# Two heads at a time in the attention stage of a two-layer transformer kernel

## Chip, core and metric

The kernel runs on one NeuronCore of one Trainium2 chip. The metric is the device time of one execution in microseconds (us). The whole model is one program; the input is one sequence of 512 tokens with 1024 features, everything in 32-bit floats.

## What is computed

Two layers of a block (feed-forward, token mixing, feed-forward), then a third block of another kind, which the change does not touch. Inside the token mixing of each layer stand two attentions over the same 512 tokens. Cut to what matters here:

```python
def masked_softmax(scores, mask):
    s = jnp.where(mask, scores.astype(jnp.float32), -jnp.inf)
    m = jnp.max(s, -1, keepdims=True)
    p = jnp.exp(s - m)
    return p / jnp.maximum(jnp.sum(p, -1, keepdims=True), 1.0)

# nsa_attention: 8 query heads of width 64 in 2 groups of 4; each group has its own keys and values
o_c = softmax(q k_c - slope * distance) v_c      # 31 compressed keys
o_s = softmax(q k_s - slope * distance) v_s      # "selected" branch: at 512 tokens all 8 blocks are selected
o_w = softmax(q k_w - slope * distance) v_w      # window of 512: all earlier tokens
out = gate[0] * o_c + gate[1] * o_s + gate[2] * o_w

# mla_attention: 8 heads, score width 64 + 32 = 96, value width 64
s = (q_nope k_nope + q_rope k_rope) * 96 ** -0.5
out = masked_softmax(s, causal) v
```

Queries are taken in four blocks of 128; query block i sees 128 * (i + 1) keys.

## The kernel before

TensorE holds the weights and the activations of all large products split into a high and a low part, so that each product is three matmuls (lines 435 to 437, or 469 to 471 with the operands' places changed). In the attention stage it works on plain 32-bit floats instead: there a matmul is recorded as two instructions, a transposition as one.

The order on each engine is written out by hand: five functions issue the instructions of TensorE, ScalarE, VectorE, GpSimd and the DMA queue, and one counting semaphore per engine (`Signal`) tells the others how far it is. Each engine takes its instructions strictly as written, so a wait holds up all that stands behind it.

The attention stage of a layer (`mix`, from line 594 on TensorE) runs over 96 units. A unit is one head, one query block i and, in the first attention (`"nsa"`), one branch `br` (0 selected, 1 window). There are 64 units of `"nsa"` (for head number hh in its group, for i, for br, for group g) and 32 of `"mla"` (for head pair j, for i, for the two heads). In loop step t TensorE does three things for three different units:

- scores of unit t (line 518 inside `scores`): one matmul, 128 queries against L = 128 * (i + 1) keys, into banks 0 to 2. In `"nsa"` two heads, one of each group, lie in the two halves of the 128 rows of `oA`; the keys `kk[:, br, g]` have zeros in the half of the other group, so the contraction runs over 128 rows though 64 count. In `"mla"` it runs over 96 rows.
- transposition of the probabilities of unit t-4 (line 524 inside `turn`): i + 1 blocks of 128 x 128, into banks 3 to 5.
- value products of unit t-6 (line 627): i + 1 matmuls with 64 stationary columns, into one half of the partitions of bank 6 or 7; in the selected branch one product with the compressed values goes before (line 623).

VectorE in loop step t scales the probabilities of unit t-4 (`scaled`: line 1478 maximum of the sum and 1, line 1480 reciprocal, line 1485 or 1483 the product) and then adds the bias to the scores of unit t-1 and takes the row minimum (`soft`, line 1471; scores carry a minus sign). At the start of each head it makes the table slope * distance (line 1616). ScalarE copies the transposed block of unit t-4 to SBUF (line 987) and then takes the exponential of unit t-1 with its row sum (line 980).

The probabilities lie in a ring of four buffers `mP`, the transposed ones in three buffers `mT`. `soft` of unit n waits until unit n-4 has been transposed; the copy of unit n waits for the value products of unit n-3. The keys `kk` are zeroed by GpSimd at the start of the stage (line 2017), and each half is filled by another engine (ScalarE through line 911, and VectorE, beside the kv copies).

## Time and profile before

| | |
|---|---|
| median of 3 runs | 3709.75 us (3704.95 to 3712.91) |
| profiled execution, its own time | 3704.14 us |
| its span in the trace | 3702.6 us |
| busy TensorE matmul / VectorE / ScalarE / GpSimd | 96% / 50% / 34% / 7% |
| attention stages | 588.03 to 758.86 us and 1857.17 to 2028.14 us |

Busy time counts how long an engine had at least one instruction under way. Matmuls overlap each other, and each is recorded longer than it occupies the array: a busy TensorE is therefore not a TensorE at its peak, and the time that a matmul costs is read from the start of one instruction to the start of the next. "PEclk" is the share of its full 2.4 GHz that TensorE was granted in a stretch. Outside the two attention stages the program is almost wholly the three-matmul products.

### The profile page before, as it was taken

How to read it: one execution, taken by the hardware profiler on the slowest of the kernel's cores; microseconds unless marked ns; L12 is line 12 of the kernel's file. 1: busy time of each engine (PE TensorE's matmuls, PEld its weight loads, DVE VectorE, ACT ScalarE, POOL GpSimd, SP SyncE). 2: the span in 40 equal slices, each digit the busy share in tenths (PEclk: the TensorE clock that was granted, in tenths of full speed). 3: DMA queues.
4: the chain of work that ended last, by engine and by line, in shares of the span. 5: the costliest groups of instructions: out<-in, count | busy, mean ns of one | idle time of the engine just before them, and what ended most of it. 6: DMA issues, size and time to landing. Idle time of an engine off the chain costs nothing.

```text
span 3702.6 us, 40550 instructions
## 1 busy us (share of the span) xinstructions
PE 3562.2 (96%) x16390; PEld 2857.7 (77%) x16390; DVE 1845.3 (50%) x3338; ACT 1249.7 (34%) x2064; POOL 273.0 (7%) x228
## 2 busy tenths in 40 slices
PE   5999999999999999998999999999999999999999
PEld 4888786678788878887766878887878777877887
DVE  6665437654565743333566443333453556454333
ACT  3222325532322232222456233222522334224322
POOL 0000210001000100011200020003110000020000
PEclk9999999999999999999999999999999999999999
DMA  5564321023465632323200322322303132222332
GB/s 216 191 217 171 100 95 45 1 72 108 137 208 204 206 112 83 108 86 108 82 21 1 101 90 94 100 93 89 94 29 111 32 103 87 66 94 74 100 100 80
DMA packets 121178, 380.54 MB, mean 103 GB/s; under 512 B 13344, under 2 KB 28064, under 8 KB 120992
## 3 DMA queue, kind: packets, MB, share of 16 engines
q1 hardware_dynamic: 120992, 377.95, 30.9%
q8 instruction: 130, 2.13, 0.2%
q14 instruction: 56, 0.46, 0.0%
HBM read 375.80 MB, written 2.10 MB: 102 GB/s over the span
## 4 chain that ended last, share of the span: by engine, by line
PE 91%; DVE 5%; ACT 3%; DMA 1%; issue 1%; POOL 0%; SPq 0%; POOLq 0%; ACTq 0%; DVEq 0%
PE ps L435 25%; PE ps L436 25%; PE ps L437 25%; PE ps L518 4%; PE ps L627 3%; PE ps L524 2%; PE ps L485 1%; PE ps L469 1%; PE ps L470 1%; PE ps L471 1%; PE ps L478 1%; DVE s_wl L1359 1%; DMA s_raw<-w 1%; PE ps L623 1%; DVE s_raw L1368 1%
## 5 line engine op out<-in xcount | busy, mean ns | idle before, releaser
L1359 DVE TENSOR_TENSOR s_wl<-s_raw,s_wh 128x1024 fp32r<-128x1024 f32 (+3 forms) x645 | 709.1, 1101 | 886.5 <-ACT s_wh L885 884.0
L435 PE MATMUL ps<-s_uh,s_wh 128*128 128x512 f32 x2760 | 1101.3, 399 | 44.3 <-DVE s_ul L1393 30.5
L436 PE MATMUL ps<-s_uh,s_wl 128*128 128x512 f32 x2760 | 1086.6, 394 | 0.0
L437 PE MATMUL ps<-s_ul,s_wh 128*128 128x512 f32 x2760 | 1085.8, 393 | 0.0
L885 ACT ACTIVATE s_wh<-s_raw 128x1024 fp32r<-128x1024 f32 (+3 forms) x645 | 588.1, 913 | 760.1 <-PE ps L437 568.2
L435 PEld LDWEIGHTS ps<-s_uh,s_wh 128*128 128x128 f32 x2760 | 526.0, 191 | 165.0 <-issue 34.0
L436 PEld LDWEIGHTS ps<-s_uh,s_wl 128*128 128x128 f32 x2760 | 526.4, 191 | 110.8 <-issue 2.3
L437 PEld LDWEIGHTS ps<-s_ul,s_wh 128*128 128x128 f32 x2760 | 525.2, 190 | 111.7
L437 PE MATMUL ps<-s_fl,s_wh 128*128 128x512 f32 x960 | 378.2, 394 | 0.0
L435 PE MATMUL ps<-s_fh,s_wh 128*128 128x512 f32 x960 | 378.2, 394 | 0.0
L436 PE MATMUL ps<-s_fh,s_wl 128*128 128x512 f32 x960 | 378.2, 394 | 0.0
L953 ACT ACTIVATE s_fh<-s_tmp 128x512 fp32r<-128x512 f32 x120 | 75.8, 632 | 417.9 <-DVE s_tmp L1450 393.0
L436 PEld LDWEIGHTS ps<-s_fh,s_wl 128*128 128x128 f32 x960 | 179.5, 187 | 44.6
L437 PEld LDWEIGHTS ps<-s_fl,s_wh 128*128 128x128 f32 x960 | 179.5, 187 | 44.4
L435 PEld LDWEIGHTS ps<-s_fh,s_wh 128*128 128x128 f32 x960 | 179.5, 187 | 44.2
L947 ACT ACTIVATE s_tmp<-ps 128x512 f32<-128x512 f32 x120 | 71.7, 598 | 359.1 <-PE ps L437 359.1
L1368 DVE CUSTOM_DVE_ANT_0 s_raw<-s_raw,s_crow 128x1024 f32<-128x1024 f32 x144 | 183.8, 1277 | 1.3 <-ACT s_crow L1311 1.3
L1999 POOL TENSOR_TENSOR s_acc<-s_x 128x512 f32<-128x512 f32 x7 | 8.6, 1226 | 1980.8 <-DVE s_x L1431 1918.5
L1450 DVE TENSOR_TENSOR s_tmp<-s_tmp,ps 128x512 f32<-128x512 f32 x88 | 60.5, 688 | 179.8 <-PE ps L437 179.7
L987 ACT ACTIVATE s_mT<-ps 128x128 f32<-128x128 f32 (+3 forms) x192 | 84.1, 438 | 138.1 <-PE ps L524 136.3
L1393 DVE TENSOR_TENSOR s_fl<-s_tmp,s_fh 128x512 fp32r<-128x512 f32 x120 | 83.1, 693 | 83.8 <-ACT s_fh L953 83.8
L1431 DVE SCALAR_TENSOR_TENSOR s_x<-ps,s_mod,s_x 128x512 f32<-128x512 f32 x80 | 60.0, 750 | 111.7 <-PE ps L437 111.7
(380 smaller groups left out, 3762.5 us busy)
## 6 DMA issues: line engine op xcount, KB each, us to landing
s_raw<-w SPq DMA_DIRECT2D x624, 512.0 KB, 3.6
s_raw<-w SPq DMA_DIRECT2D x96, 192.0 KB, 2.4
s_raw<-w SPq DMA_DIRECT2D x64, 256.0 KB, 2.6
s_raw<-w SPq DMA_DIRECT2D x19, 128.0 KB, 2.1
s_x<-x SPq DMA_DIRECT2D x1, 2048.0 KB, 10.5
out<-s_x SPq DMA_DIRECT2D x8, 256.0 KB, 2.2
s_raw<-w SPq DMA_DIRECT2D x4, 420.0 KB, 3.9
s_crow<-crow SPq DMA_DIRECT2D x2, 512.0 KB, 3.6
```

The source lines that it names most:

```text
L435: TE.matmul(o, w_hi(i, k), h, start=first, stop=False)
L436: TE.matmul(o, w_lo(i, k), h, start=False, stop=False)
L437: return TE.matmul(o, w_hi(i, k), l, start=False, stop=last)
L518: TE.matmul(o[:, 0:L], q, k, start=True, stop=True).then_inc(*s_pe.up(("ps", ("S", g))))
L524: ins = TE.transpose(o[:, sl(j)], p[:, sl(j)], ident)
L627: ins = TE.matmul(o, v, mT[n % 3][:, sl(j)], start=kind == "mla" and j == 0, stop=j == i and (kind == "mla" or br == 1))
L885: SC.activation(wh[slot[t]][:, 0:n], raw[t % NRAW][:, 0:n], ACT.Copy).then_inc(*s_hi.up(("hi", t)))
L953: SC.activation(fh[:, j, :], s[:], ACT.Copy).then_inc(*s_act.up(("hh", st, jj)))
L987: SC.activation(T[n % 3][:, 0:L], bank(("T", (st, n)))[:, 0:L], ACT.Copy).then_inc(*s_act.up(("pt", (st, n)), frees=("T", (st, n))))
L1359: V.tensor_tensor(wl[w][:, 0:n], raw[t % NRAW][:, 0:n], wh[w][:, 0:n].bitcast(F32), SUB).then_inc(*s_lo.up(("lo", t)))
L1368: V.tensor_tensor_reduce(raw[i % NRAW][:], raw[i % NRAW][:], crow[:], 1.0, 0.0, MUL, ADD, mod[:, o:o + 1]).then_inc(*s_dve.up(("raw", i)))
L1393: V.tensor_tensor(dst, src, hi.bitcast(F32), SUB).then_inc(*s_dve.up(key))
```

## The change

The list of 96 units becomes a list of 48 pairs. A pair is the two heads that stood behind one another before: the two groups' heads in `"nsa"`, two neighbouring heads in `"mla"`.

- TensorE, in loop step t: both scores of pair t, then the transpositions of pair t-2, then the value products of pair t-3. In `"nsa"` each score contracts over 64 rows only, head g over rows 64g to 64g+63, into a bank of its own. The value products of the two heads alternate block by block; each head writes its own half of the partitions.
- `kk` loses its zero halves: half the size, no memset, one copy by ScalarE over 128 partitions, and VectorE's two copies are gone.
- VectorE: `soft` of both heads of pair t, then for pair t-1 one maximum and one reciprocal over two columns, and two products.
- ScalarE: exponentials of pair t-1, then copies of pair t-2.
- The slope tables are made by GpSimd, in four buffers instead of two, two heads ahead; GpSimd begins with them when TensorE has finished the latent products.
- Rings: six probability buffers (two of them are `tmp[0]`, `tmp[1]`), four transposed ones (`acc` is one), four banks for scores, two for transpositions.

```diff
+def attention_pairs():
+    u = [("nsa", hh, i, br) for hh in range(4) for i in range(4) for br in range(2)]
+    return u + [("mla", j, i, 0) for j in range(4) for i in range(4)]
...
-            kk = sb(c1, "kk", [128, 2, 2, 512])
+            kk = sb(c1, "kk", [128, 2, 512])
...
+                slope = [sb(c2, f"slope{i}", [128, 512]) for i in range(2)] + [tmp[2], tmp[3]]
+                mP = [sb(c2, f"mP{i}", [128, 512]) for i in range(4)] + [tmp[0], tmp[1]]
+                mT = [sb(c2, f"mT{i}", [128, 512]) for i in range(3)] + [acc]
...
@@ tensor_engine @@
+            for t in range(len(pairs) + 3):
+                if t < len(pairs):
+                    kind, h, i, br = pairs[t]
+                    L = 128 * i + 128
...
+                    o = [take(("S", (st, 2 * t + g)), 2 * (t % 2) + g) for g in range(2)]
+                    for g in range(2):
+                        if kind == "nsa":
+                            q, k = oA[64 * g:64 * g + 64, h, sl(i)], kk[64 * g:64 * g + 64, br, 0:L]
+                        else:
+                            q, k = mq[0:96, 2 * h + g, sl(i)], mk[0:96, 2 * h + g, 0:L]
+                        TE.matmul(o[g][:, 0:L], q, k, start=True, stop=True).then_inc(*s_pe.up(("ps", ("S", (st, 2 * t + g)))))
+                if 0 <= t - 2 < len(pairs):
+                    for n in (2 * t - 4, 2 * t - 3):
+                        turn((st, n), 4 + n % 2, mP[n % 6], 128 * pairs[t - 2][2] + 128)
+                if 0 <= t - 3 < len(pairs):
...
+                    if kind == "nsa" and br == 0:
+                        for g in range(2):
+                            TE.matmul(o[g], vc[:, h, 64 * g:64 * g + 64], pcT[:, i, g, :], start=True, stop=False)
                     for j in range(i + 1):
+                        for g in range(2):
+                            pe.wait_ge(*s_act["pt", (st, n + g)])
+                            at = 128 * br + 64 * g if kind == "nsa" else 128 * h + 64 * g
+                            v = (vt if kind == "nsa" else mv)[:, j, at:at + 64]
+                            ins = TE.matmul(o[g], v, mT[(n + g) % 4][:, sl(j)], start=kind == "mla" and j == 0, stop=j == i and (kind == "mla" or br == 1))
...
@@ scalar_engine @@
+            for t in range(len(pairs) + 3):
+                if 0 <= t - 1 < len(pairs):
...
+                    for n in (2 * t - 2, 2 * t - 1):
+                        act.wait_ge(*s_dve["s", (st, n)])
+                        SC.activation(p[:, 0:L], p[:, 0:L], ACT.Exp, bias=two(n, 0), scale=-1.0, accum_out=two(n, 1)).then_inc(*s_act.up(("e", (st, n))))
+                if 0 <= t - 2 < len(pairs):
+                    for n in (2 * t - 4, 2 * t - 3):
+                        act.wait_ge(*s_pe["ps", ("T", (st, n))])
+                        if n > 3:
+                            act.wait_ge(*s_pe["pv", (st, n - 4)])
+                        SC.activation(mT[n % 4][:, 0:L], bank(("T", (st, n)))[:, 0:L], ACT.Copy).then_inc(*s_act.up(("pt", (st, n)), frees=("T", (st, n))))
...
@@ vector_engine @@
+            for t in range(len(pairs) + 1):
+                if t < len(pairs):
...
+                    for g in range(2):
...
+                        dve.wait_ge(*s_pe["ps", ("S", (st, n))])
+                        if n > 5:
+                            dve.wait_ge(*s_pe["ps", ("T", (st, n - 6))])
+                        V.tensor_tensor_reduce(mP[n % 6][:, 0:L], bank(("S", (st, n)))[:, 0:L], bias, 1.0, 3.0e38, ADD, MIN, two(n, 0)).then_inc(
...
+                if t > 0:
...
+                    dve.wait_ge(*s_act["e", (st, n + 1)])
+                    V.tensor_scalar(mfew[:, c0 + 4:c0 + 6], mfew[:, c0 + 2:c0 + 4], 1.0, None, MAX).then_inc(*s_dve.up(("max", (st, n))))
...
+                    V.reciprocal(mfew[:, c0 + 6:c0 + 8], mfew[:, c0 + 4:c0 + 6]).then_inc(*s_dve.up(("rec", (st, n))))
...
+                    for g in range(2):
...
+                            V.tensor_scalar(p[:, 0:L], p[:, 0:L], two(n + g, 3), gt[:, i, k:k + 1], MUL, MUL).then_inc(*s_dve.up(("p", (st, n + g))))
...
@@ pool_engine @@
-            PO.memset(kk[:], 0.0).then_inc(*s_pool.up(("zk", st)))
...
+            pool.wait_ge(*table(f"dist {st}"))
+            pool.wait_ge(*s_pe["latent", st])
...
+            for h in range(4):
+                for g in range(2):
+                    if h > 1:
+                        pool.wait_ge(*s_dve["slope used", st, h - 2])
+                    PO.tensor_scalar(slope[2 * (h % 2) + g][:], dist[:], -SLOPE[4 * g + h], None, MUL).then_inc(*s_pool.up(("slope", st, h, g)))
```

How the order moves. TensorE, first head of `"nsa"`, around the first scores against 512 keys, before (L518 scores, L524 transpositions, L623 and L627 value products; `x3` is how many matmuls stand in a row):

```order
2181 L518 MATMUL ps<-s_kk,s_oA 128x512
2182 L524 MATMUL ps<-s_cst,s_mP 128x128 x3
2183 L627 MATMUL ps<-s_mT,s_vt 64x128 x2
2184 L518 MATMUL ps<-s_kk,s_oA 128x512
2185 L524 MATMUL ps<-s_cst,s_mP 128x128 x3
2186 L627 MATMUL ps<-s_mT,s_vt 64x128 x2
2187 L518 MATMUL ps<-s_kk,s_oA 128x512
2188 L524 MATMUL ps<-s_cst,s_mP 128x128 x3
2189 L623 MATMUL ps<-s_pcT,s_vc 64x128
2190 L627 MATMUL ps<-s_mT,s_vt 64x128 x3
```

And in the changed kernel (L608 scores, L517 transpositions, L621 and L627 value products; `s_tmp` and `s_acc` are the added ring buffers):

```order
2169 L608 MATMUL ps<-s_kk,s_oA 128x512 x2
2170 L517 MATMUL ps<-s_cst,s_mP 128x128 x6
2171 L627 MATMUL ps<-s_mT,s_vt 64x128
2172 L627 MATMUL ps<-s_acc,s_vt 64x128
2173 L627 MATMUL ps<-s_mT,s_vt 64x128
2174 L627 MATMUL ps<-s_acc,s_vt 64x128
2175 L608 MATMUL ps<-s_kk,s_oA 128x512 x2
2176 L517 MATMUL ps<-s_cst,s_tmp 128x128 x6
2177 L621 MATMUL ps<-s_pcT,s_vc 64x128 x2
2178 L627 MATMUL ps<-s_mT,s_vt 64x128 x6
```

Each kind of work now stands for two heads in a row, and the value products of the two heads alternate.

VectorE in the same head at the scores against 384 keys, before (the two ISA rows are the bias addition and the reading of its row minimum):

```order
503 L1471 ISA s_mP,s_mfew<-ps,s_slope 128x384
504 L1471 ISA s_mfew 128x1
505 L1478 TENSOR_SCALAR s_mfew<-s_mfew 128x1
506 L1480 RECIPROCAL s_mfew<-s_mfew 128x1
507 L1485 TENSOR_SCALAR s_mP<-s_mP,s_mfew,s_gt 128x256
```

And in the changed kernel:

```order
486 L1628 ISA s_mP,s_mfew<-ps,s_slope 128x384
487 L1628 ISA s_mfew 128x1
488 L1628 ISA s_mP,s_mfew<-ps,s_slope 128x384
489 L1628 ISA s_mfew 128x1
490 L1636 TENSOR_SCALAR s_mfew<-s_mfew 128x2
491 L1638 RECIPROCAL s_mfew<-s_mfew 128x2
492 L1644 TENSOR_SCALAR s_mP<-s_mP,s_mfew,s_gt 128x256 x2
```

Two additions stand first, then one maximum and one reciprocal for the pair before, then its two products. Before, a unit was scaled three steps after its scores' bias was added; now a pair is scaled one step after.

## Rows read from the trace of the kernel before

**Rows 1.** Page, chain that ended last, its shares of the span by line:

```profile
PE ps L435 25%; PE ps L436 25%; PE ps L437 25%; PE ps L518 4%; PE ps L627 3%; PE ps L524 2%; PE ps L485 1%; PE ps L469 1%; PE ps L470 1%; PE ps L471 1%; PE ps L478 1%; DVE s_wl L1359 1%; DMA s_raw<-w 1%; PE ps L623 1%; DVE s_raw L1368 1%
```

**Rows 2.** Windows, both attention stages: length, busy PE, PEld, DVE, ACT, POOL, clock, DMA share, GB/s:

```profile
588.03:758.86 170.83, 169.72 (x978) 113.28 (x976) 112.97 (x488) 98.76 (x296) 0.00 (x0) 1.00 0.01 3
1857.17:2028.14 170.97, 169.78 (x978) 113.30 (x976) 112.96 (x488) 98.76 (x296) 0.00 (x0) 1.00 0.01 3
```

**Rows 3.** Waits in 588:759, us in total, times, longest:

```profile
ACT s_mT L987 <- PE ps L524: 68.1, 85, 1.3
DVE s_mP L1471 <- PE ps L524: 45.6, 68, 1.3
```

**Rows 4.** Timeline of TensorE in "mla": start, duration of the merged row, instruction:

```profile
714.52 0.70 PE L518 MATMUL ps<-s_mk,s_mq 96*128 96x256 f32 x2
715.06 0.60 PE L524 MATMUL ps<-s_cst,s_mP 128*128 128x128 f32 x4
715.59 0.87 PE L627 MATMUL ps<-s_mT,s_mv 128*64 128x128 f32 x6
716.39 0.70 PE L518 MATMUL ps<-s_mk,s_mq 96*128 96x256 f32 x2
...
722.20 1.13 PE L518 MATMUL ps<-s_mk,s_mq 96*128 96x512 f32 x2
723.16 0.38 PE L524 MATMUL ps<-s_cst,s_mP 128*128 128x128 f32 x2
```

**Rows 5.** Timeline of TensorE, last value products of the first stage:

```profile
757.07 1.86 PE L627 MATMUL ps<-s_mT,s_mv 128*64 128x128 f32 x22
```

**Rows 6.** Timeline of TensorE, matmuls on parts of the array elsewhere:

```profile
476.81 3.72 PE L545 MATMUL ps<-s_raw,s_mq 128*31 128x128 f32 x64
...
3190.63 1.09 PE L809 MATMUL ps<-s_gv,s_gE 64*64 64x128 f32 x28
```

**Rows 7.** Timeline of VectorE, a unit of 128 keys, then the end of the stage:

```profile
590.44 0.28 DVE L1471 CUSTOM_DVE_ANT_0 s_mP<-ps,s_slope 128x128 f32<-128x128 f32 x1
...
590.65 0.15 DVE L1478 TENSOR_SCALAR s_mfew<-s_mfew 128x1 f32<-128x1 f32 x1
...
752.56 0.69 DVE L1471 CUSTOM_DVE_ANT_0 s_mP<-ps,s_mmask 128x512 f32<-128x512 f32 x1 [0.22 <-PE ps L524]
...
753.18 0.15 DVE L1478 TENSOR_SCALAR s_mfew<-s_mfew 128x1 f32<-128x1 f32 x1
...
753.56 0.42 DVE L1483 TENSOR_SCALAR s_mP<-s_mP,s_mfew 128x384 f32<-128x384 f32 x1
753.89 0.15 DVE L1478 TENSOR_SCALAR s_mfew<-s_mfew 128x1 f32<-128x1 f32 x1
```

**Rows 8.** Timeline of ScalarE at the end of the stage:

```profile
752.73 0.71 ACT L980 ACTIVATE s_mP<-s_mP,s_mfew 128x512 f32<-128x512 f32 x1
...
753.43 0.48 ACT L987 ACTIVATE s_mT<-ps 128x384 f32<-128x384 f32 x1
753.81 0.72 ACT L980 ACTIVATE s_mP<-s_mP,s_mfew 128x512 f32<-128x512 f32 x1
```

**Rows 9.** Timeline, one hand-over from TensorE to ScalarE:

```profile
590.67 0.30 PE L524 MATMUL ps<-s_cst,s_mP 128*128 128x128 f32 x1 [0.25 <-ACT s_mP L980]
...
591.01 0.28 ACT L987 ACTIVATE s_mT<-ps 128x128 f32<-128x128 f32 x1 [0.43 <-PE ps L524]
```

**Rows 10.** Groups of GpSimd by shape: busy us, mean ns, idle before:

```profile
L2061 POOL TENSOR_TENSOR s_gqk<-s_ghs 128x512 f32<-128x512 f32 x4 | 4.0, 1042 | 333.5 <-ACT s_ghs L911 333.5
...
L2019 POOL MEMSET s_vc<- 128x512 f32 x2 | 1.1, 525 | 0.0
```

**Rows 11.** Timeline of VectorE at the stage's start:

```profile
588.23 0.43 DVE L1616 TENSOR_SCALAR s_slope<-s_dist 128x512 f32<-128x512 f32 x1 [3.07 <-PE ps L471]
```

**Rows 12.** Windows ahead of the first stage, columns as in rows 2:

```profile
568.00:572.00 4.00, 1.46 (x7) 0.86 (x5) 2.56 (x5) 3.67 (x7) 0.85 (x1) 0.99 0.00 0
572.00:576.00 4.00, 3.77 (x10) 3.07 (x11) 3.71 (x7) 3.42 (x7) 2.00 (x2) 0.58 0.59 173
```

More of the change, by code:

```diff
@@ L622, in mix @@
+                if 0 <= t - 3 < len(pairs):
+                    n = 2 * t - 6
+                    kind, h, i, br = pairs[t - 3]
+                    both = ("o", st, kind, h)
+                    if i == 0 and br == 0:
+                        take(both, 6 + h % 2)
+                    o = [bank(both)[64 * g:64 * g + 64, sl(i)] for g in range(2)]
                     if kind == "nsa" and br == 0:
-                        TE.matmul(o, vc[:, h, 64 * g:64 * g + 64], pcT[:, i, g, :], start=True, stop=False)
```

107 lines of the change are left out of this document (38 added, 69 removed).

## The prediction, made before the changed kernel ran

> **What bounds the kernel now.** I read the chain that ended last first: three products of the large matmuls hold 75% of it, and the four lines of the attention stages (518, 627, 524, 623) together 10% [rows 1]. The windows then give the stages: 170.8 and 171.0 us, at the full clock, almost no DMA, and TensorE busy for 169.7 us of them, VectorE for 113.0 and ScalarE for 98.8 [rows 2]. The list of waits says which way the waiting goes: ScalarE waits 68.1 us for TensorE's transpositions and VectorE 45.6 us for the same line, which frees its ring of probabilities [rows 3]. So TensorE alone sets these stages, and only what its instructions cost there counts; about 341.8 us of the span can be touched.
>
> **What a unit costs on TensorE.** From start to start in "mla" [rows 4]: a score against 2 blocks of keys takes 0.54 us and against 4 blocks 0.96, so 0.21 a block and 0.12 for its first weights. Four transpositions take 0.53: two more of them lengthen the merged row from 0.38 to 0.60, so 0.11 each, and 0.09 are left. Six value instructions (3 blocks) take 0.80: at the same 0.11 each, 0.14 are left. I read the 0.09 and the 0.05 in the 0.14 as the change of the array's shape (128 columns to 64 and back) and the first load behind it. Mean over 1 to 4 blocks: score 0.65, transpositions 0.27 + 0.09, value products 5 x 0.11 + 0.14 = 0.69; together 1.70. The selected branch adds two instructions of compressed values, 0.22, to half the "nsa" units: 0.11 on average. 64 x 1.81 + 32 x 1.70 = 170.2 us, against 170.8 and 171.0 measured. The model is good to half a per cent, and 0.7 us are left for filling and emptying the pipeline.
>
> **What runs side by side.** The change pays only if matmuls on different parts of the array overlap. Three rows say that they do. The last three value products of the stage, 6 + 8 + 8 instructions on alternating column halves, begin at 757.07 [rows 5] and the stage ends at 758.86: 1.79 us, where one after another they need 22 x 0.11 + 3 x 0.05 = 2.57. Line 545 does 64 instructions on two column strips in 3.72 us, 0.058 each; line 809 does 28 on four quarters (both row halves, both column halves) in 1.09 us, 0.039 each [rows 6]. Each of these moves 128 columns, as the value instructions at 0.11 do. So two column halves cost as one, and with row halves too it is cheaper still. What no row shows is two row halves with 128 stationary columns each: bounds are one score's time (0.65) and two (1.19). I take one, since line 809 is the nearest row.
>
> **The change on TensorE, pair by pair.** "nsa": two scores side by side 0.65; change of shape and first load 0.15; five transpositions 0.55; change 0.09; value products side by side 0.69; compressed values 0.11 on average; 2.24 x 32 = 71.7 us. Three changes of shape for two heads where there were four. "mla": the scores contract over 96 rows and cannot share the array, 0.65 + 0.54 (the second one's weights load beneath the first); transpositions 0.55 + 0.09; value products 0.69; 2.52 x 16 = 40.3 us. Together 112.0 us, 58.2 fewer than 170.2.
>
> **What the other engines then need.** ScalarE loses nothing: 98.8 us busy [rows 2]. VectorE: bias addition 0.21 us at one block and 0.62 at four, maximum and reciprocal 0.38 together, scaling 0.33 at three blocks [rows 7]. A pair is 2 x 0.415 + 0.38 + 2 x 0.33 = 1.87, so 90 us for 48. The slope tables (8 x 0.43 [rows 11]) leave it. Both engines fit under 112, but at 88% and 80%, so local waits appear. The loop that matters: pair t's scores end, VectorE adds both biases, then scales pair t-1, whose transpositions TensorE wants after transposing t-2, the value products of t-3 and the scores of t+1. A hand-over costs 0.34 - 0.11 = 0.23 us [rows 9]; I take 0.3 for both ways. At the first pair against 384 keys TensorE has 0.59 + 0.36 + 0.84 = 1.79 us of work for the interval, VectorE needs 2 x 0.48 + 0.38 + 0.40 + 0.3 = 2.04: 0.25 us late. The same count over an "nsa" head of eight steps gives two such steps and a trifle, 0.6 us; over an "mla" group of four steps one, 0.3 us. 4 x 0.6 + 4 x 0.3 = 3.6; I take 4. Bounds: 0, and 16 if a quarter of a microsecond and more is lost in every step.
>
> **Filling.** GpSimd makes the tables when VectorE did before, from 588.23. No row has a one-input GpSimd operation of this size: below stands the memset of 128x512 with 0.525 us, above the two-input product with 1.04 [rows 10]. I take 0.6, near the memset, since one input is to be read. Two tables: 589.4. Then the second head's bias 0.2, the next pair's biases 0.4, exponentials beneath, 0.38 + 0.35: the first transposition can start near 591.0. TensorE has by then three score pairs, 1.3 of 3.0 us: 1.7 idle, and some 0.8 in the next step. 2.5 us; with the upper bound 3.4. The Trainium skill (GPSIMD Engine Reference, 1. Specifications) says that GpSimd's SBUF interface is shared with VectorE, which contends with two-input and two-port VectorE instructions. The first tables are made while VectorE idles, later ones a head ahead, so by that rule the sum stays.
>
> **Emptying.** The last pair's way (both biases, exponentials behind two copies at 0.7 us each [rows 8], scaling, transposition, copy) is longer than TensorE's remaining work by about 1.3 us. **Clock.** In the trace, after four us in which TensorE was busy for 1.46, the next four had a mean clock of 0.58 [rows 12]. The fill is such a spot; 3.4 us at half speed would cost up to 1.7, I take 1.0 (bounds 0 and 1.7).
>
> The removed memset and the copies of `kk` lie far from the stage, beneath matmuls that do not wait for them: nothing. Weights: five raw tiles are in place before the stage and no DMA moves in it, so nothing is late behind it.
>
> **Sum.** 112.0 + 4 + 2.5 + 1.3 + 1.0 = 120.8 us a stage, 50.1 fewer than 170.9; two stages 100.2. The profiled execution took 3704.1 us (span 3702.6): 3603.9. The median shown is 5.6 us above it: 3609.
>
> **Rivals.**
> (a) The row halves do not overlap in the scores, only the columns do. For it: no row shows the case; against: line 809. Costs 0.54 x 32 x 2 = 35 us: 3644.
> (b) The softmax chain becomes the bound. Here VectorE stands still until both exponentials are done and only then scales, in every step: 1.87 plus half of ScalarE's 98.8 / 48 = 1.0 is 2.9 a step, 139 + 5 a stage, 27 saved, 54 in all: 3656. Against it: the exponentials of pair t-1 run while VectorE adds the biases of pair t; for it: ScalarE starts them only behind two copies that wait for TensorE. The Trainium skill (TensorEngine Tiling, PSUM Bottleneck) warns that tiling speeds TensorE but not the evacuation of PSUM, which may become the bottleneck. By that rule it would be this rival; the trace has 98.8 us busy for the fuller engine against my 120.8, which speaks against a full bound.
> (c) Neither kind overlaps, because each head's loads and products are taken in order: 17 for scores and 5 x 0.11 x 48 + 3.5 = 30 for values, 47 a stage, 94 in all: 3703 to 3712, no change. Rows 5 and 6 speak against it.
> (d) Slower: TensorE's clock falls to 1.2 GHz in the stages because of the new short waits. Some 95 of the 112 us are streaming, which would double: 95 a stage, 3609 + 190 = 3799. It decides from about half of a stage at the lower level (48 us) on. For it: rows 12 show a fall after an idle spell. Against: the waits I expect past the fill are 0.3 us, and in the stage before the clock stayed 1.00 [rows 2].
>
> **How the numbers follow.** The forecast has 0.70; its own range is 3594 (no local waits and no clock loss: 5 us less a stage, and the measured spread) to 3630 (local waits of 12 instead of 4 a stage, GpSimd's upper bound). (a) 0.07, (b) 0.12, (c) 0.03, (d) 0.04, and 0.04 for a mixture that is faster than before. The range 3592 to 3656 leaves out (c), (d) and part of (b). A change under 0.2% (7 us) cannot be told from none here. Faster: 0.70 + 0.07 + 0.12 + 0.04 = 0.93; same 0.03; slower 0.04.
>
> **What the profile will show.** Right: stages of about 121 us; merged score rows of "nsa" as long for four instructions as for two before; value rows of two heads at 0.055 us an instruction; ScalarE and VectorE near 99 and 91 us busy with waits for TensorE left; the clock below 1.00 at most at the start. Wrong: scores of 1.2 us a pair (a); TensorE waiting for `mP` or `mT` in nearly every step, half a microsecond each (b); value products still 0.11 apart (c); a clock of 0.5 inside the stage (d). The prediction fails as a whole if the stages stay above 145 us.

## The result and the profile after

The changed kernel takes 3608.75 us (median of 4 runs, 3606.39 to 3609.13), the kernel before 3707.35 us in the same session (4 runs, 3697.67 to 3712.91). The ratio is 0.9734, with a 95% interval of 0.9718 to 0.9751: faster by 2.7%. The prediction said 3609.

The page after, total busy times and the chain by line:

```profile
PE 3456.9 (96%) x16390; PEld 2780.6 (77%) x16390; DVE 1801.2 (50%) x3126; ACT 1238.8 (34%) x2064; POOL 294.7 (8%) x242
...
PE ps L428 26%; PE ps L429 25%; PE ps L430 25%; PE ps L608 2%; PE ps L517 2%; PE ps L627 1%; PE ps L462 1%; PE ps L478 1%; PE ps L464 1%; PE ps L463 1%; PE ps L471 1%; DVE s_wl L1367 1%; DMA s_raw<-w 1%; DVE s_raw L1376 1%; ACT s_wh L886 1%
```

Against [rows 1] the attention lines have shrunk from 4, 3, 2 and 1% to 2, 2 and 1%. The two stages as windows, columns as in [rows 2]:

```profile
585.56:708.62 123.06, 115.80 (x977) 75.56 (x977) 94.04 (x384) 93.46 (x296) 12.21 (x8) 0.99 0.01 4
1805.69:1928.79 123.10, 116.96 (x977) 76.08 (x977) 94.16 (x384) 92.97 (x295) 11.59 (x8) 0.97 0.01 4
```

Each runs from its first score to the first matmul behind its last value product. They were 170.83 and 170.97 and are 123.06 and 123.10: 95.6 us together. The span fell by 95.0 (3702.6 to 3607.6), so the rest of the kernel together changed by 0.6 us. TensorE has as many instructions as before (977 for 978) and is busy for 116 us instead of 170. So it is with instructions that run side by side: the count stays and the busy time falls.

One pair in TensorE's timeline after (start, duration of the merged row, instruction):

```profile
600.85 1.13 PE L608 MATMUL ps<-s_kk,s_oA 64*128 64x512 f32 x4
601.91 0.88 PE L517 MATMUL ps<-s_cst,s_tmp 128*128 128x128 f32 x6
602.72 0.44 PE L621 MATMUL ps<-s_pcT,s_vc 128*64 128x128 f32 x4
602.99 0.82 PE L627 MATMUL ps<-s_mT,s_vt 128*64 128x128 f32 x12
603.74 0.49 PE L608 MATMUL ps<-s_kk,s_oA 64*128 64x128 f32 x4
```

Four score instructions against 512 keys take 1.06 us to the next line's start; two took 0.96 before [rows 4]; the 0.10 more come back in E10, where no change of shape follows the score. In the records behind the row the two heads' first instructions start at 600.853 and 600.860, 7 ns apart, and their second ones 0.526 later, again 7 ns apart. Twelve value instructions take 0.75 us, 0.063 each; from one step to the next four more of them add 0.22 us (groups of 12, 16 and 20 take 0.81, 1.02 and 1.24), so an instruction costs 0.055, as forecast, and the rest is the change of shape.

The waits in 590:707 (us in total, times, longest):

```profile
ACT s_mT L1061 <- PE ps L517: 20.0, 36, 1.2
...
DVE s_mP L1628 <- PE ps L608: 12.3, 17, 1.7
PEld ps L517 <- ACT s_mP L1054: 11.9, 21, 1.0
```

ScalarE still waits for TensorE's transpositions, but 20.0 us instead of 68.1 [rows 3] (this window leaves out the filling); VectorE no longer waits for them at all, but 12.3 us for scores. New is the third row: the load ahead of a transposition waits for the softmax chain, 21 times. Most of it lies beneath a running matmul; TensorE stands still 7.3 us in the stage (123.06 less 115.80).

Where TensorE's time went, from the starts of all its instructions in the first stage: each group counts from its own first start to the start of the next group, its waits included, and the sum is the stage. "E5" is the experiment below in which the value products of the kernel before have full width.

| first stage, us | before | after | E5 |
|---|---|---|---|
| "nsa" scores | 42.4 | 30.0 | 36.6 |
| transpositions | 35.4 | 34.4 | 27.0 |
| value products | 72.5 | 38.7 | 61.3 |
| "mla" scores | 20.6 | 20.0 | 18.3 |
| sum | 170.9 | 123.1 | 143.2 |

### The profile page after: what moved, and what is told of

The parts are those of the page before. It is cut to its first block, busy times and chain, and to the rows that moved or that the text cites. A ratio compares the mean times of both kernels' runs of the same rounds, so it can differ in the third digit from the quotient of the medians.

```text
span 3607.6 us, 40374 instructions
## 1 busy us (share of the span) xinstructions
PE 3456.9 (96%) x16390; PEld 2780.6 (77%) x16390; DVE 1801.2 (50%) x3126; ACT 1238.8 (34%) x2064; POOL 294.7 (8%) x242
## 4 chain that ended last, share of the span: by engine, by line
PE 89%; DVE 6%; ACT 4%; POOL 1%; issue 1%; DMA 1%; SPq 0%; POOLq 0%; ACTq 0%; DVEq 0%
PE ps L428 26%; PE ps L429 25%; PE ps L430 25%; PE ps L608 2%; PE ps L517 2%; PE ps L627 1%; PE ps L462 1%; PE ps L478 1%; PE ps L464 1%; PE ps L463 1%; PE ps L471 1%; DVE s_wl L1367 1%; DMA s_raw<-w 1%; DVE s_raw L1376 1%; ACT s_wh L886 1%
## 5 line engine op out<-in xcount | busy, mean ns | idle before, releaser
L428 PEld LDWEIGHTS ps<-s_fh,s_wh 128*128 128x128 f32 x960 | 179.5, 187 | 44.6
L2029 POOL TENSOR_TENSOR s_acc<-s_acc,s_tmp 128x512 f32<-128x512 f32 x42 | 84.1, 2002 | 3.3
```

Of the source, the lines that this page charges most:

```text
L428: TE.matmul(o, w_hi(i, k), h, start=first, stop=False)
L2029: PO.tensor_tensor(acc[:], acc[:], t[:], ADD).then_inc(*s_pool.up(("sq", st, m), ("sq", st)))
```

## The experiments

Every kernel was timed against the kernel before on the same chip. The intervals of E1, E4, E9, E10 and E11 overlap that of the changed kernel, so the readings rest on the stages' lengths, each from one profiled execution. One thing disturbs these: in a short stretch of most stages TensorE was granted the lower of its two clock levels (1.2 of 2.4 GHz), and the stretch is not equally long in every kernel. The last column estimates what that cost at most: the stage's length times what its mean granted clock, taken to three places, lacks to 1. Differences between kernels of 2 us a stage and less have to be read with it. The summary first, then each experiment with its reading.

| kernel | median us | ratio to before (95%) | stages us | of it lower clock, at most |
|---|---|---|---|---|
| before | 3707.4 | 1 | 170.8, 171.0 | 0, 0 |
| changed | 3608.8 | 0.9734 (0.9718 to 0.9751) | 123.1, 123.1 | 1.7, 3.4 |
| E1 full rows | 3624.7 | 0.9778 (0.9737 to 0.9819) | 131.8, 129.9 | 1.7, 0 |
| E2 full columns | 3657.9 | 0.9843 (0.9797 to 0.9890) | 141.9, 141.2 | 3.4, 3.4 |
| E3 both full | 3660.1 | 0.9866 (0.9823 to 0.9909) | 146.5, 145.6 | 1.7, 1.7 |
| E4 first tables on VectorE | 3608.1 | 0.9724 (0.9690 to 0.9758) | 121.8, 122.8 | 1.7, 3.4 |
| E5 before, full columns | 3649.6 | 0.9854 (0.9834 to 0.9873) | 143.1, 143.2 | 0, 0 |
| E6 heads in turn | 3628.4 | 0.9795 (0.9779 to 0.9812) | 132.0, 130.9 | 3.4, 3.4 |
| E7 shallow rings | 3637.3 | 0.9810 (0.9795 to 0.9825) | 138.1, 135.9 | 5.1, 3.4 |
| E8 single softmax | 3622.8 | 0.9774 (0.9759 to 0.9789) | 129.6, 128.8 | 3.4, 3.4 |
| E9 scores of two pairs | 3619.4 | 0.9767 (0.9750 to 0.9783) | 128.7, 128.9 | 5.1, 5.1 |
| E10 row-half transpositions | 3596.8 | 0.9707 (0.9690 to 0.9725) | 119.1, 118.6 | 3.4, 3.4 |
| E11 one step later | 3602.0 | 0.9722 (0.9707 to 0.9738) | 120.3, 119.4 | 3.4, 3.4 |
| E12 E4, E10 and E11 together | 3584.8 | 0.9676 (0.9659 to 0.9692) | 111.5, 111.5 | 3.4, 1.7 |

**E1, full rows.** The scores contract over 128 rows of a zero-padded `kk`, as before:

```diff
-    q, k = oA[64 * g:64 * g + 64, h, sl(i)], kk[64 * g:64 * g + 64, br, 0:L]
+    q, k = oA[:, h, sl(i)], kk[:, br, g, 0:L]
```

> The two scores of an "nsa" pair contract over 128 rows again (kk with its zero halves, the memset and the two copies back), everything else as changed. Theory (row halves run side by side): the second score of a pair costs its own time again, 0.54 us on average; 32 pairs x 2 stages = 35 us, less up to 6 us of short waits for the softmax chain that the longer score hides: +29 to +35 us, 3638 to 3644, stages of 138 to 141 us. In the rows the first instructions of the two scores start 0.2 us or more apart for one block of keys, not 0.007. Rival (row halves give nothing; the pair order, the rings or the joint maxima made the gain): 0, 3609.

**E2, full columns.**

```diff
-    o = [bank(both)[64 * g:64 * g + 64, sl(i)] for g in range(2)]
+    o = [bank(both)[:, sl(i)] for g in range(2)]
...
-    at = 128 * br + 64 * g if kind == "nsa" else 128 * h + 64 * g
-    v = (vt if kind == "nsa" else mv)[:, j, at:at + 64]
+    at = 128 * br if kind == "nsa" else 128 * h
+    v = (vt if kind == "nsa" else mv)[:, j, at:at + 128]
```

(and the product with the compressed values likewise)

> Each head's value product uses all 128 columns of values and writes all 128 partitions, so both heads' sums land on top of each other in the output of this kernel; the count, order and streamed columns of the instructions are unchanged. Theory (column halves run side by side): an instruction costs 0.109 us again where it costs half. Per stage 32 x 3.0 x 0.22 (nsa with the compressed product) + 16 x 2.5 x 0.22 = 29.9 us more, 60 in both, less up to 12 of regained short waits: +48 to +60, 3657 to 3669. Rival (the gain of the value products came from alternating heads behind one another's loads, not from disjoint columns): 0 to +5, 3609 to 3614.

**E3, both edits.**

> Both: full rows for the scores, full columns for the value products (the two heads' sums on top of each other, as above). Theory: the two gains add, +95 us less up to 14 of regained waits: 3690 to 3704, stages near 164 to 170; what is left of the change (fewer shape changes, two waits fewer per pair on VectorE) is worth 3 to 17 us against the kernel before's 3707. Rival (pairing of the softmax and deeper rings carry a good part): 3670 or less, since they remain.

Windows of the first stage of E1, E2 and E3, in this order, one kernel in each fence:

```profile
589.65:721.43 131.78, 126.99 (x977) 88.20 (x976) 96.77 (x384) 93.14 (x296) 12.21 (x8) 0.99 0.02 4
```

```profile
587.60:729.53 141.93, 136.45 (x977) 109.40 (x977) 94.74 (x384) 93.07 (x296) 12.21 (x8) 0.98 0.01 4
```

```profile
588.70:735.17 146.47, 141.70 (x977) 119.17 (x976) 96.09 (x384) 92.89 (x296) 12.21 (x8) 0.99 0.01 3
```

In E1 the two scores no longer start together. Four instructions against 512 keys take 1.83 us to the next line's start (606.63 to 608.46) where the changed kernel takes 1.06, and the second head's first instruction starts 0.96 us behind the first head's:

```profile
606.63 1.98 PE L609 MATMUL ps<-s_kk,s_oA 128*128 128x512 f32 x4
```

The rivals of E1 and E2 do not hold: both overlaps are real, and taking them away costs 15.5 us (E1, both stages; 18.9 if the clock column is taken off) and 37.0 us (E2; 35.3). But my sizes were too large, 29 to 35 and 48 to 60, and the two together cost 46.0 (E3) instead of 81 to 95. E3's rival had the right number, 3670 or less, but E5 will show that it had the wrong cause. In E1 the "nsa" score rows grew by 12.1 us in the first stage (30.0 to 42.1) and not by the 17.3 of 32 x 0.54, and the transpositions behind them shrank from 34.4 to 31.6. In E2 the value products grew by 26.4 (38.7 to 65.1), while transpositions fell to 29.2 and both kinds of scores together by 2.4. Something paid back wherever a full-shape matmul now stood next to another one. E5 was made to find it.

The medians of E2 and E3 also hold something foreign. In E3's profiled run 40 us far behind the second stage ran at a mean granted clock of 0.54 (E2 has 0.62 in 3130:3180), where the changed kernel's stretch with the same work has 0.87:

```profile
3150.00:3190.00 40.00, 40.00 (x147) 32.28 (x147) 3.87 (x6) 5.23 (x8) 3.47 (x4) 0.54 0.03 7
```

```profile
3100.00:3140.00 40.00, 40.00 (x218) 33.56 (x219) 8.97 (x22) 7.18 (x10) 9.14 (x8) 0.87 0.08 20
```

The fastest run of each kernel gives 35.4 us for E2 (3641.8 against 3606.4) and 44.6 for E3 (3651.0), in line with the stages.

**E4, first tables on VectorE.**

```diff
+    if t == 0:
+        V.tensor_scalar(slope[g][:], dist[:], -SLOPE[4 * g], None, MUL).then_inc(*s_dve.up(("slope", st, 0, g)))
...
-            for h in range(4):
+            for h in range(1, 4):
```

> VectorE makes the two slope tables of head 0 itself (0.42 us each as in the kernel before), GpSimd the other six. Theory (the filling of the stage is set by GpSimd's 1.53 us per table): TensorE's idle spell of 3.1 us at the start of the first stage shrinks to about 1, the second's of 2.2 to about 0.5; 2 x (1.53 - 0.42) = 2.2 us a stage at most in the first and less in the second, and perhaps 1 to 3 us of the half-clock spell: -3 to -7 us, 3602 to 3606. Rival (something else, such as the first exponentials behind the hand-over, sets the filling): 0 to -1.

The changed kernel's filling, TensorE and GpSimd timelines and then two windows:

```profile
585.56 0.71 PE L608 MATMUL ps<-s_kk,s_oA 64*128 64x128 f32 x8
589.33 0.70 PE L608 MATMUL ps<-s_kk,s_oA 64*128 64x256 f32 x4 [3.06 <-DVE s_mfew L1628]
590.64 0.66 PE L517 MATMUL ps<-s_cst,s_mP 128*128 128x128 f32 x2 [0.61 <-DVE s_mP L1644]
```

```profile
585.79 3.07 POOL L2087 TENSOR_SCALAR s_slope<-s_dist 128x512 f32<-128x512 f32 x2 [11.29 <-PE ps L464]
```

```profile
586.00:590.00 4.00, 0.94 (x10) 0.41 (x6) 1.24 (x10) 1.53 (x7) 3.84 (x3) 1.00 0.25 68
590.00:594.00 4.00, 3.39 (x17) 1.88 (x16) 3.69 (x19) 3.05 (x15) 2.02 (x2) 0.57 0.01 4
```

Two tables take GpSimd 3.07 us, 1.53 each. With VectorE making them TensorE's 3.06 + 0.61 us of idle became 1.05 + 1.22: the first gap is GpSimd's, the second then falls to the softmax chain, since the first transposition needs two tables, two biases and two exponentials whoever makes them. The stages are shorter by 1.3 and 0.3 us, and the clock still falls (0.57 in the four us behind). My -3 to -7 us did not come: the stages give -1.6 over both, and the median is the same within the measurement. The cause of the first gap is shown, its size as a gain was wrong.

**E5, the kernel before with full columns.** No overlap, no pairs; only the value products of the kernel before are widened, so that its "nsa" units consist of 128x128 matmuls alone:

```diff
-                    o = bank(pair)[64 * g:64 * g + 64, sl(i)]
+                    o = bank(pair)[:, sl(i)]
...
-                        v = vt[:, j, 128 * br + 64 * g:128 * br + 64 * g + 64] if kind == "nsa" else mv[:, j, 64 * h:64 * h + 64]
+                        v = vt[:, j, 128 * br:128 * br + 128] if kind == "nsa" else mv[:, j, 128 * (h // 2):128 * (h // 2) + 128]
```

> The kernel before (heads one after another, single softmax, rings of four and three), but its value products use all 128 columns, so that every matmul of an "nsa" unit has the same 128x128 shape; both heads' sums land on top of each other. Theory (formed after the full-rows and full-columns runs: a matmul whose shape differs from its predecessor's costs time of its own, and the stage before contains 29.9 us of this: score 6.1 and 2.0, transpositions 8.6, values 13.2 us above 0.109 us an instruction): the stages fall from 170.9 to 142 to 149 us although no instruction leaves, in all 43 to 58 us less than before, near 3655. Rival (pairing, joint maxima and deeper rings made the full-shape version 24 us a stage shorter than before): stages stay at 168 to 172, 3707.

TensorE in "mla", the stretch that answers to [rows 4]:

```profile
691.80 0.60 PE L518 MATMUL ps<-s_mk,s_mq 96*128 96x256 f32 x2
692.24 0.60 PE L524 MATMUL ps<-s_cst,s_mP 128*128 128x128 f32 x4
692.68 0.83 PE L627 MATMUL ps<-s_mT,s_mv 128*128 128x128 f32 x6
693.35 0.60 PE L518 MATMUL ps<-s_mk,s_mq 96*128 96x256 f32 x2
```

Start to start, score, transpositions and values take 0.44, 0.44 and 0.67 us, where [rows 4] have 0.54, 0.53 and 0.80 for as many instructions that stream the same data. A wider stationary operand made each group faster, because its neighbours have the same shape. The stage fell from 170.8 to 143.1 us with no instruction less; the theory said 142 to 149, the rival 168 to 172. The 27.7 us over 96 units with two changes of shape each are 0.14 us a change on average; neither kernel spent any of the stage at the lower clock. (96 rows beside 128 rows cost nothing: 0.44 is four times 0.11.) The Trainium skill (TensorEngine Tiling (Array Packing), Tiling Modes, Key Properties) says that switching the tiling mode, though not the tile within one, drains TensorE. The trace agrees that a switch costs time, 0.14 us; whether that is a drain, or weights of the new shape that cannot be loaded early, it does not tell.

So the kernel before paid some 28 us a stage for 64-column value products that overlapped with next to nothing. E5 alone, with no overlap and no pairs, is 55 us shorter over both stages, where the change is 95.6 (its output mixes the two heads' sums, so it is a measurement and no kernel to use); the changed kernel is 20.0 us a stage below it. And E3, which is the changed kernel without its overlaps, is with 146.5 us no shorter than E5's 143.1: pairs, joint maxima and deeper rings bring nothing that shows while TensorE's matmuls run one after another, and the 24 us that E3 is below the kernel before are not more than the changes of shape that E5 found. The change still pays for changes of shape, three in an "nsa" pair and two in an "mla" pair, 128 a stage instead of 192.

**E6, heads in turn.**

```diff
-                    for j in range(i + 1):
-                        for g in range(2):
+                    for g in range(2):
+                        for j in range(i + 1):
```

> The changed kernel, the value products of head 0 all ahead of those of head 1 instead of alternating. Theory A (instructions start in order, and one waits only for its predecessors on the same columns): only neighbours overlap, so nearly the whole gain of the columns goes: per stage 29.9 us less the 0.22 us of the one overlapping pair of instructions (48 x 0.22 = 10.5), some 17 to 20 us more, 3642 to 3650. Theory B (the two streams are queued apart and overlap whatever the order): 0 to +2 us a stage, 3609 to 3613.

TensorE's timeline, eight value instructions of head 0 (`mT`) and then eight of head 1 (`acc`):

```profile
653.30 0.76 PE L627 MATMUL ps<-s_mT,s_vt 128*64 128x128 f32 x5
653.79 0.32 PE L627 MATMUL ps<-s_acc,s_vt 128*64 128x128 f32 x1
653.89 0.27 PE L627 MATMUL ps<-s_mT,s_vt 128*64 128x128 f32 x1
653.95 0.27 PE L627 MATMUL ps<-s_acc,s_vt 128*64 128x128 f32 x1
654.00 0.27 PE L627 MATMUL ps<-s_mT,s_vt 128*64 128x128 f32 x1
654.06 0.27 PE L627 MATMUL ps<-s_acc,s_vt 128*64 128x128 f32 x1
654.11 0.27 PE L627 MATMUL ps<-s_mT,s_vt 128*64 128x128 f32 x1
654.17 0.71 PE L627 MATMUL ps<-s_acc,s_vt 128*64 128x128 f32 x5
```

Neither theory holds; the truth lies between. Head 1's first instruction, the ninth in the program, starts at 653.79, when head 0's fifth has started and three of head 0's have not. The last four of head 0 overlap, the others don't. It is so in every group of the stage: with six instructions a head, head 1 starts behind head 0's third, with eight behind its fifth, 6 ns later. What is lost is n - 4 instructions of 0.109 us where a head has n = 6 or 8, and nothing where it has 2 or 4: 1.5 instructions on average, 0.16 us a pair, 7.9 a stage. Measured: 8.9 and 7.8, or 7.2 and 7.8 without the clock column. Alternating the heads is worth 15 to 17 us of the change's gain. It also explains [rows 5], the overlap that the kernel before had in its last groups of six, eight and eight: there too the next head's first instruction starts 6 ns behind the third of six and the fifth of eight. So that an engine takes its instructions strictly as written does not hold for the starts of TensorE's matmuls.

**E7, shallow rings.**

```diff
-                        if n > 5:
-                            dve.wait_ge(*s_pe["ps", ("T", (st, n - 6))])
+                        if n > 3:
+                            dve.wait_ge(*s_pe["ps", ("T", (st, n - 4))])
```

(with `mP[n % 4]` for `mP[n % 6]` and `mT[n % 3]` for `mT[n % 4]` throughout)

> The changed kernel with four probability tiles and three transposed ones instead of six and four. VectorE can then add pair t's biases only when TensorE has transposed pair t-2: hand-over 0.23 + two biases + 0.38 + first scaling + hand-over 0.1 must fit between two groups of transpositions: 2.3 us at three blocks against a step of 2.4, 3.1 against 3.1 at four. Theory (TensorE sets the stage, the rings only cover): +3 to +12 us a stage, 3615 to 3633. Rival (the rings are worth nothing, softmax has room enough): 0, 3609. Rival (the rings carry much of the gain): over +15 a stage, 3640 and more.

Waits in 590:722:

```profile
ACT s_mT L1061 <- PE ps L627: 31.8, 44, 1.3
DVE s_mP L1628 <- PE ps L517: 31.4, 46, 1.7
PEld ps L517 <- ACT s_mP L1054: 21.3, 23, 2.0
```

The wait of [rows 3], VectorE for the transpositions that free its ring, is back with 31.4 us in 46 waits, and now it counts, because behind it TensorE's loads wait 21.3 us instead of 11.9. The first row is the other ring: ScalarE's copies wait 31.8 us for the value products that free the transposed tiles. The run narrows both rings at once and does not tell which of them costs more. The stages are 15.1 and 12.8 us longer (11.7 and 12.8 without the clock column), at or past the top of my theory's 3 to 12: without the deeper rings about a quarter of the gain is gone (24 to 28 of 95.6 us), so they are no mere cover.

**E8, single softmax.** Maximum and reciprocal once per head:

```diff
-                    dve.wait_ge(*s_act["e", (st, n + 1)])
-                    V.tensor_scalar(mfew[:, c0 + 4:c0 + 6], mfew[:, c0 + 2:c0 + 4], 1.0, None, MAX).then_inc(*s_dve.up(("max", (st, n))))
+                    for g in range(2):
+                        dve.wait_ge(*s_act["e", (st, n + g)])
+                        V.tensor_scalar(two(n + g, 2), two(n + g, 1), 1.0, None, MAX).then_inc(*s_dve.up(("max", (st, n + g))))
```

> The changed kernel with maximum and reciprocal made for each head apart, as before the change. VectorE gets 0.38 us more a pair, 18 us a stage: 94 + 18 = 112 us busy of 123; the first head's scaling no longer waits for the second exponential. Theory (the joint maxima are needed once TensorE is down to 123 us): steps of few blocks, where VectorE's fixed costs weigh most, become VectorE's: +4 to +12 us a stage, 3617 to 3633. Rival (VectorE still hides beneath TensorE): 0 to +1 a stage, 3609 to 3611.

Its first stage:

```profile
588.89:718.53 129.64, 120.32 (x977) 76.09 (x976) 106.22 (x480) 95.35 (x296) 12.11 (x8) 0.97 0.01 4
```

VectorE has 96 instructions and 12.2 us more; the stages are 6.6 and 5.7 us longer (4.9 and 5.7 without the clock column), and the transposition groups hold it (34.4 to 41.8 us). An engine at 94 us of 123 is not hidden from what is added to it: nearly half of the 12.2 us came through. That is the theory's 4 to 12.

**E9, scores of two pairs together.**

```diff
-                if t < len(pairs):
-                    kind, h, i, br = pairs[t]
+                for t1 in (t, t + 1) if t % 2 == 0 and t < len(pairs) else ():
+                    kind, h, i, br = pairs[t1]
```

> The changed kernel, but TensorE issues the scores of two pairs together in every second step (the order S S T V T V for two pairs where it is S T V S T V). Theory (each change of the matmul's shape costs about 0.14 us, entering the row halves about 0.19): six changes per two "nsa" pairs become five, one entry into the row halves less, 16 x 0.19 = 3 us a stage, nothing in "mla": -4 to -6 us in both stages, 3603 to 3605. Rival (the stage is held by the softmax chain, which this does not shorten, or the four score banks come free too late): 0 to +6.

My theory fails and the rival's direction holds, but 5.6 and 5.8 us a stage are 11.4 in both, twice the rival's upper bound of 6; by the clock column up to 5.1 of them are the lower clock, which lasted longer than in the changed kernel in both stages. In VectorE's timeline the joint maximum waits for ScalarE, and then in TensorE's a transposition for VectorE's scaled probabilities:

```profile
615.41 0.17 DVE L1636 TENSOR_SCALAR s_mfew<-s_mfew 128x2 f32<-128x2 f32 x1 [1.09 <-ACT s_mP L1054]
```

```profile
618.38 0.73 PE L517 MATMUL ps<-s_cst,s_tmp 128*128 128x128 f32 x4 [0.90 <-DVE s_tmp L1644]
```

Scores that come in bursts of two pairs leave the chain with nothing to do and then with too much. Whether the saved change of shape was gained beneath that cannot be read apart.

**E10, row-half transpositions.** Each transposition in two of 64 rows, the first half of both heads to bank 4 and the second to bank 5:

```diff
+                        for j in range(pairs[t - 2][2] + 1):
+                            for r in range(2):
+                                a = slice(64 * r, 64 * r + 64)
+                                c = 256 * (n % 2) + 64 * j
+                                ins = TE.transpose(o[r][:, c:c + 64], mP[n % 6][a, sl(j)], ident[a, a])
```

> The changed kernel with each 128x128 transposition cut into two of 64 rows: query rows 0 to 63 of both heads go to bank 4, rows 64 to 127 to bank 5, and ScalarE's copy reads both banks in one instruction, once both heads are transposed. Theory (row halves overlap, and a stream of 64 columns costs half of one of 128): the pure streaming of the transpositions falls from 26.8 us a stage towards 13.4; in "nsa" they now have the shape of the scores (32 x 0.14 = 4.6 us less), in "mla" a change of shape comes in (16 x 0.14 = 2.2 us more); the copies start up to 0.3 us later. With VectorE at 94 and ScalarE at 93 us busy, 108 to 117 us a stage instead of 123: -12 to -30 us, 3579 to 3597. Rival (an instruction has a floor of its own near 0.109 us, or VectorE's chain holds the stage already): 121 to 125 a stage, 3605 to 3613.

TensorE's timeline, then VectorE's of the same two us:

```profile
654.11 1.13 PE L611 MATMUL ps<-s_kk,s_oA 64*128 64x512 f32 x4
655.07 0.54 PE L620 MATMUL ps<-s_cst,s_mP 64*128 64x64 f32 x12
...
657.52 0.37 PE L620 MATMUL ps<-s_cst,s_tmp 64*128 64x64 f32 x5 [0.27 <-DVE s_tmp L1657]
```

```profile
655.27 0.69 DVE L1641 CUSTOM_DVE_ANT_0 s_mP<-ps,s_tmp 128x512 f32<-128x512 f32 x1
...
655.89 0.69 DVE L1641 CUSTOM_DVE_ANT_0 s_mP<-ps,s_tmp 128x512 f32<-128x512 f32 x1
...
656.90 0.87 DVE L1657 TENSOR_SCALAR s_tmp<-s_tmp,s_mfew,s_gt 128x384 f32<-128x384 f32 x2
657.68 0.68 DVE L1641 CUSTOM_DVE_ANT_0 s_mP<-ps,s_tmp 128x512 f32<-128x512 f32 x1
```

Six blocks go through in 0.47 us, the change of shape behind them included, where the changed kernel needs 0.81 (601.91 to 602.72), and the score row in front takes 0.96 instead of 1.06 to the next start, since no change of shape follows it. The transposition groups fell from 34.4 to 25.2 us, but the stages only by 4.0 and 4.5 (5.7 and 4.5 without the clock column), about half of that: the "nsa" score groups grew to 32.7, "mla" scores to 21.5, values to 39.8, and TensorE's idle time from 7.3 to 10.7. VectorE works from 655.27 to 657.68 without a stop and delivers a pair's probabilities only behind the next pair's two biases. 119.1 and 118.6 us lie between my theory's range (108 to 117) and the rival's (121 to 125): the faster transpositions are real, and I left out that the chain takes half of them back.

**E11, one step later.** Transpositions of t-3 and value products of t-4, with eight probability tiles:

```diff
-                if 0 <= t - 2 < len(pairs):
-                    for n in (2 * t - 4, 2 * t - 3):
-                        turn((st, n), 4 + n % 2, mP[n % 6], 128 * pairs[t - 2][2] + 128)
+                if 0 <= t - 3 < len(pairs):
+                    for n in (2 * t - 6, 2 * t - 5):
+                        turn((st, n), 4 + n % 2, mP[n % 8], 128 * pairs[t - 3][2] + 128)
```

> The changed kernel with transpositions and value products one step later (S of t, T of t-3, V of t-4) and eight probability tiles instead of six, in the room that the smaller kk left. Theory (2.4 us a stage of waits longer than 0.15 us stand outside filling and emptying, before transpositions whose probabilities VectorE has just been late with, and the transposition rows are about 2 us longer than their streams and changes of shape need): these waits go, the pipeline empties one step later: 119 to 121 us a stage instead of 123, -4 to -8 us, 3601 to 3605. Rival (VectorE's or ScalarE's throughput is short in the steps of four blocks, whatever the lag): -2 to 0 us.

120.3 and 119.4 us, as the theory said; the median 3602.0 too. The rival had at most 2 us and does not hold: these waits were latency, which a longer lag hides, and not throughput.

**E12, E4, E10 and E11 together.**

> What the earlier runs point to together: transpositions in two row halves, head 0's tables on VectorE, and transpositions and value products one step later with eight probability tiles. Theory: from 118.9 us a stage with row-half transpositions, less about 5 us of waits outside filling and emptying, less about 1 us of filling: 111 to 115 us a stage, 3580 to 3590 in all. Rival (VectorE, 94 us busy, and ScalarE, 93, are short in the steps of four blocks): 116 to 119, 3592 to 3600.

```profile
585.92:697.47 111.55, 104.03 (x1218) 70.59 (x1217) 93.03 (x386) 91.67 (x296) 9.28 (x6) 0.97 0.02 5
```

111.5 us in both stages, 3584.8 us in all: 24 us below the changed kernel, and its interval (0.9659 to 0.9692) lies wholly below the changed kernel's. One by one the parts gave 0.8 us a stage (E4), 4.2 (E10) and 3.2 (E11), 8.2 in sum; together they give 11.6. Part of the difference is the clock: without that column it is 9.9 in sum against 11.6. The rest fits the reading that the later step takes away waits on which E10's faster transpositions had been spent: TensorE is idle for 7.5 us of this stage (111.55 less 104.03) where E10 has 10.7, and the shorter filling explains only some 1.4 of that (2.27 in E4, 3.67 in the changed kernel). That is argued from these sums, and no run took the three parts two at a time.

## Why the prediction was right, point by point

**The bound and the overlap** held. Row halves of two heads start 7 ns apart, column halves 6 to 7 ns apart; rivals (a) and (c) are excluded by E1, E2 and the timeline, and (d) by the clock (0.99 and 0.97 in the windows).

**TensorE's 112.0 us** was right, in sum and in its parts. If each kind of group is given the shortest time that it took anywhere in the stage, a pair costs 2.19 us in "nsa" and 2.54 in "mla", where the forecast had 2.24 and 2.52: 110.8 us in both stages. E5 shows why it fitted although I misread the pieces. The 0.12, 0.09 and 0.14 that I read off [rows 4] as "first weights" and "change of the array's shape" fell by 0.10, 0.09 and 0.13 when the shapes became equal, so nearly all of it is change of shape. I kept these pieces in the pairs, about as much as their two or three changes cost, and so had the right total. What had no name in my sum is what made the expectations of E1 to E3 too large: I priced the return to full shapes by streams alone and forgot that uniform shapes give changes back.

**Local waits**: 4 us forecast. They can be read from the trace of the changed kernel, where a group takes longer than the shortest of its kind. Between 603 and 703 us, past the filling, such groups (those at least 0.06 us longer) have 4.5 us in sum, and the same stretch of the second stage has 4.5 too. The place that I named, the first pair against 384 keys, has 0.28 us (0.25 forecast), and TensorE waits there for VectorE's probabilities:

```profile
612.99 0.92 PE L608 MATMUL ps<-s_kk,s_oA 64*128 64x384 f32 x4
614.11 0.73 PE L517 MATMUL ps<-s_cst,s_mP 128*128 128x128 f32 x4 [0.21 <-DVE s_mP L1644]
```

A group of four "mla" steps has 0.29 (0.3 forecast). An "nsa" head has 1.2 to 1.4 where I counted 0.6: pairs against 512 keys are late as well. The mechanism was right, and this term was half of what it should have been in "nsa"; it came out near because the first head's waits lie hidden in the filling. E11, which gives the chain one more step, brings 2.7 and 3.7 us (4.4 and 3.7 without the clock column).

**Filling** was mis-sized: 2.5 us forecast, 3.7 and 2.7 measured. GpSimd took 1.53 us for a table (1.50 for the first, with VectorE idle) where I took 0.6 with bounds 0.525 and 1.04 [rows 10]; the upper bound, a two-input product, was not one. The nearest row by shape was of another operation, and the scalar product cost three times the memset. By my own steps two tables of 1.5 us would have made 4.3; in the second stage GpSimd began 0.6 us ahead of the first score (1805.07 and 1805.69), in the first 0.2 behind it.

**Clock**: 1.0 forecast, with bounds 0 and 1.7. The first stage has 1.7 (four us at 0.57 in the window 590:594), the second up to 3.4, outside the bounds: the spell behind the filling is longer there, though the idle time ahead of it is shorter.

```profile
1809.00:1813.00 4.00, 3.52 (x20) 1.88 (x16) 3.65 (x19) 3.11 (x14) 2.30 (x2) 0.52 0.00 0
1813.00:1817.00 4.00, 4.00 (x20) 1.72 (x16) 2.50 (x10) 1.96 (x9) 0.00 (x0) 0.63 0.00 0
```

**Emptying**: 1.3 forecast, 1.1 measured in both (0.81 and 0.33). With 112.0 for TensorE's work the first stage is 112.0 + 3.7 + 1.1 + 1.7, and 4.6 are left for local waits; the second 112.0 + 2.7 + 1.1 + 3.4, and 3.9 are left.

**The sum, and luck.** Both stages come to 123.1 where the sum had 120.8, 4.6 us too few over both: filling, clock and the "nsa" waits were each too small. The profiled execution was 3609.1, where the sum said 3603.9. That the median (3608.75) still came out within a microsecond of 3609 is luck: the forecast put the median 5.6 us above the profiled execution, as it was for the kernel before, and for the changed kernel the two are 0.4 us apart. The two errors cancel.

**VectorE and ScalarE**: forecast 90 and 98.8 us busy, measured 94 and 93. Rival (b) does not hold for the changed kernel, but it is near: E8 shows that 12 us more on VectorE cost about 6 a stage, E7 that shallower rings cost about 14, and E10 that half of what a faster TensorE gains goes to the chain. The Trainium skill (TensorEngine Tiling (Array Packing), PSUM Bottleneck) warned that the emptying of PSUM may become the bottleneck once TensorE is faster. That did not happen with this change; in E10 the next limit is near, but it is the whole softmax chain, of which the copies out of PSUM are one part.

## What to carry to other kernels

Splitting the array pays only where the tiles overlap: side by side an instruction cost 0.055 us instead of 0.109 here, but every change of shape cost 0.14 us, so 64-column matmuls that overlap with nothing, between 128-column ones, were dearer than full-width ones (E5). Put the instructions of the tiles alternately in the program, and give the engines behind them room (rings, one more step of lag) in the same change, since an engine that was hidden at 113 of 171 us is not hidden at 94 of 123. And when the bound of a step is read from a neighbouring row, take one of the same operation: here the scalar product on GpSimd was outside both neighbours.

## What the runs showed of the hardware

- Between float32 matmuls that use 128 and 64 columns of the array a change costs TensorE 0.14 us on average (E5: 27.7 us in 192 changes); from 96 to 128 rows it costs nothing. From 64 rows to 128 it costs about 0.10 (a score group of 1.06 us in the changed kernel and 0.96 in E10).
- TensorE starts matmuls out of program order when they are on different column halves: in E6 the ninth instruction starts before the sixth, seventh and eighth. On row halves too: the scores of the second head start 7 ns behind the first head's first instruction and 0.53 us ahead of its second. The Trainium skill (TensorE: Matmul & The Clock Gate, Part 3: Packing small matmuls) says that matmuls start and end strictly in program order; here the starts in the trace differ, and the measurement decides (the ends are modelled and show nothing). In E6 it passes three waiting instructions and no more, so an order that alternates is still better.
- A 128x512 product of float32 with a scalar took 1.53 us on GpSimd on average (16 of them), and 0.43 on VectorE [rows 11].
- One ScalarE instruction that reads two PSUM banks (E10) costs what one bank costs. Groups of its copies by shape in 600:700, the changed kernel and then E10:

```profile
L1061 ACT ACTIVATE s_mT<-ps 128x512 f32<-128x512 f32 x15 | 8.7, 597 | 6.2 <-PE ps L517 6.2
```

```profile
L1072 ACT ACTIVATE s_mT<-ps 128x512 f32<-128x512 f32 x15 | 8.5, 597 | 5.3 <-PE ps L620 5.2
```
